# Rows of the residual stream for the second layer's out stage: 32x32 transposes on VectorE and SBUF transfers in place of TensorE transposes

## What is computed

```python
x = ffn_sublayer(x, mod_x, 0, norm_w[l, 0], ffn1_w_up[l], ffn1_w_down[l])
yx = modulated_norm(x, norm_w[l, 1], mod_x, 1)
px = split_projection(yx @ w_in[l])       # k, v, q, g, conv b/c/x, two gates
o_x = bidir_retention(qx, kx, vx, ret_log_decay[l], s_f, s_b)
# mixer_merge:
y_ret = (silu(g) * head_rmsnorm(o)) @ w_ret_out
y_conv = (conv_b * short_conv(conv_c * conv_x, conv_w)) @ w_conv_out
merged = sigmoid(gate_ret) * y_ret + sigmoid(gate_conv) * y_conv
x = x + mod_x[:, :, 5] * (merged @ w_out[l])
x = ffn_sublayer(x, mod_x, 2, norm_w[l, 2], ffn2_w_up[l], ffn2_w_down[l])
return rmsnorm(x, final_norm_w)
```

## Time and profile before

| | us |
|---|---|
| median of 3 runs (lowest, highest) | 2116.18 (2116.07, 2116.65) |
| profiled execution, its own time | 2116.01 |
| its span in the trace | 2114.2 |
| TensorE busy | 2105.1 |
| VectorE busy | 1442.1 |
| ScalarE busy | 805.6 |
| granted TensorE clock, share of full speed | 0.999 |

### The profile page before, as it was taken

How to read it: one execution, slowest core, us unless ns; L and a number is a source line. 1 busy time by engine, 2 the same in 40 slices (tenths; PEclk the granted TensorE clock), 3 DMA queues, 4 the chain that set the end, 5 groups by cost and what they waited for, 6 DMA issues and landing times.

```text
span 2114.2 us, 26101 instructions
## 1 busy us (share of the span) xinstructions
PE 2105.1 (100%) x10451; PEld 1782.0 (84%) x10451; DVE 1442.1 (68%) x1992; ACT 805.6 (38%) x1196; POOL 0.2 (0%) x4
## 2 busy tenths in 40 slices
PE   9999999999999999999999999999999999999998
PEld 7888888888888888898888888888888898888887
DVE  5687877668588773577777777733335688778765
ACT  5322222456322322342222233222223665557654
POOL 0000000000000000000000000000000000000000
PEclk9999999999999999999999999999999999999999
DMA  8665555431555653355555545433333446765664
GB/s 272 210 178 164 171 166 157 139 90 41 159 155 159 189 150 93 92 148 173 174 168 164 170 137 148 142 93 100 92 100 107 131 122 198 207 210 154 188 190 145
DMA packets 461628, 319.65 MB, mean 151 GB/s; under 512 B 19758, under 2 KB 436934, under 8 KB 461126
## 3 DMA queue, kind: packets, MB, share of 16 engines
q1 hardware_dynamic: 439708, 244.95, 40.5%
q10 hardware_dynamic: 21800, 73.03, 10.6%
HBM read 312.16 MB, written 1.05 MB: 148 GB/s over the span
## 4 chain that ended last, share of the span: by engine, by line
PE 99%; DVE 0%; ACT 0%; issue 0%; DVEq 0%
PE bank L657 22%; PE bank L659 22%; PE bank L658 22%; PE bank L668 9%; PE bank L671 5%; PE bank L990 4%; PE bank L696 2%; PE bank L734 1%; PE bank L754 1%; PE bank L753 1%; PE bank L752 1%; PE bank L700 1%; PE bank L738 1%; PE bank L1034 0%; PE bank L1035 0%; PE bank L1036 0%
## 5 line engine op out<-in xcount | busy, mean ns | idle before, releaser
L1606 DVE TENSOR_TENSOR LO<-RAW,HI 128x1024 fp32r<-128x1024 f32 (+1 forms) x431 | 518.3, 1207 | 358.7 <-ACT HI L1132 358.4
L657 PE MATMUL bank<-Y,HI 128*128 128x512 f32 (+1 forms) x1416 | 550.1, 388 | 0.0
L659 PE MATMUL bank<-Y,LO 128*128 128x512 f32 (+1 forms) x1416 | 549.2, 388 | 0.0
L658 PE MATMUL bank<-Y,HI 128*128 128x512 f32 (+1 forms) x1416 | 549.2, 388 | 0.0
L1132 ACT ACTIVATE HI<-RAW 128x1024 fp32r<-128x1024 f32 (+1 forms) x431 | 438.2, 1039 | 216.3 <-DMA RAW<-in_w_in_dram 58.2
L658 PEld LDWEIGHTS bank<-Y,HI 128*128 128x128 f32 x1416 | 265.9, 188 | 54.9 <-issue 0.5
L657 PEld LDWEIGHTS bank<-Y,HI 128*128 128x128 f32 x1416 | 265.9, 188 | 54.8 <-issue 0.5
L659 PEld LDWEIGHTS bank<-Y,LO 128*128 128x128 f32 x1416 | 265.9, 188 | 54.6
L1617 DVE SCALAR_TENSOR_TENSOR MODACC<-MODRAW,SC,MODACC 128x1024 f32<-128x1024 f32 x224 | 277.2, 1279 | 2.4 <-DMA MODRAW<-in_w_mod_dram 2.0
L1331 ACT ACTIVATE TMP<-bank 128x512 f32<-128x512 f32 x66 | 39.4, 598 | 414.9 <-PE bank L659 334.2
L668 PE MATMUL bank<-Y,HI 128*128 128x512 f32 x720 | 181.0, 393 | 0.0
(11 more groups left out here) (293 smaller groups left out, 2537.6 us busy)
## 6 DMA issues: line engine op xcount, KB each, us to landing
RAW<-in_ffn_w_up_dram SPq DMA_DIRECT2D x170, 512.0 KB, 4.1
MODRAW<-in_w_mod_dram ACTq DMA_DIRECT2D x128, 512.0 KB, 4.3
RAW<-in_w_in_dram SPq DMA_DIRECT2D x128, 512.0 KB, 4.1
RAW<-in_ffn_w_down_dram SPq DMA_DIRECT2D x66, 512.0 KB, 3.6
RAW<-in_ffn_w_down_dram SPq DMA_DIRECT2D x24, 384.0 KB, 3.2
WM<-in_w_mod_dram SPq DMA_DIRECT2D x16, 512.0 KB, 9.1
RAW<-in_w_ret_out_dram SPq DMA_DIRECT2D x16, 512.0 KB, 4.4
RAW<-in_w_conv_out_dram SPq DMA_DIRECT2D x16, 512.0 KB, 3.7
```

The lines of the kernel that those rows point to most:

```text
L657: mm(bank, hi, X[:, k, 0, cols], start=first, stop=False)
L658: mm(bank, hi, X[:, k, 1, cols], start=False, stop=False)
L659: return mm(bank, lo, X[:, k, 0, cols], start=False, stop=end)
L1606: V_.tensor_tensor(weights(v, 1), raw_weights(v), weights(v, 0).bitcast(F32), ALU.subtract).then_inc(lo_done, 1)
```

## The change

The transposes on TensorE and the four copies on ScalarE go. Instead VectorE transposes `H[:, n, 0:256]` within 32x32 blocks, in the conv stage behind the merge of each role-0 unit, into `turned` (spare columns of blocks 12 to 15 of `S`). A 32x32 transpose leaves each block in its own group of 32 partitions, so transfers must move it: 64 DMA transfers on SP's queue, each from one group of 32 partitions (q) to another (b), four ahead of the load of each gates unit from 8 to 23. They signal `rows_landed`, for which SP waits ahead of the load of the out stage's unit 7 (whose place overlaps `turned`), and VectorE at the start of the out stage.

```diff
-            if s.kind == "out":
-                s.ht = [p.acc(4 + i) for i in range(4)]
...
+        turned = spare(S, 12, 4).rearrange("p j a n -> p (j a) n")
+
+        def row_blocks(t, b, q, e):
+
+            src = turned[32 * q:32 * q + 32, :, (4 * t + b) * 32:(4 * t + b) * 32 + 32]
+            rows = spare(S, 16 + 2 * t, 2)[32 * b:32 * b + 32]
+            dst = rows.rearrange("p c a n -> p (c a) n")[:, :, P * e + 32 * q:P * e + 32 * q + 32]
+            return dst, src.rearrange("p (m e) n -> p e m n", e=2)[:, e, :, :]
...
+                        if s.kind == "out" and cc == 7:
+                            sp.wait_ge(rows_landed, 16 * 64)
                         load(s.u + cc, w.rearrange("(k p) n -> p k n", p=P)[:, cc:cc + 1, :])
...
+                        if s.wide and s.kind == "gates" and 8 <= cc < 24:
+                            if cc == 8:
+                                sp.wait_ge(blocks_turned, KT)
+                            for q in range(4):
+                                dst, src = row_blocks((cc - 8) // 8, (cc - 8) // 2 % 4, q, cc % 2)
+                                sp.dma_start(dst, src).then_inc(rows_landed, 16)
                         w, base = parts[cc % len(parts)]
                         load(s.u + cc, block_of(w, 0, KT, base + (cc // len(parts)) * P))
...
-                        if s.wide and cc in (8, 12, 16, 20):
-                            i = cc // 4 - 2
-                            a = follows(s).ht[i]
-                            bank_wait(pe, a)
-                            for m in range(4):
-                                ins = nc.tensor.transpose(B[a.bank][:, m * P:(m + 1) * P],
-                                                          H[:, 4 * (i % 2) + m, TCOLS[i // 2]], ident)
-                            ins.then_inc(ht_turned, 1)
...
-                        if s.wide and cc in (9, 13, 17, 21):
-                            i = cc // 4 - 2
-                            act.wait_ge(ht_turned, i + 1)
-                            a = follows(s).ht[i]
-                            A(xrow(i // 2, i % 2), halves2(B[a.bank][:]), ACT.Copy).then_inc(drained[a.bank], 1)
...
                     dve.wait_ge(dense, 2)
+                    dve.wait_ge(rows_landed, 16 * 64)
                     split_upto(nx.u + 3)
...
                             merge(s, cc, TMP[:, 0, HALF:2 * HALF])
+                            V_.transpose(turned[:, n, :], H[:, n, 0:NX]).then_inc(blocks_turned, 1)
```

More of the change, by code:

```diff
@@ L416, in build @@
         gates_set, gate_rows, final_landed = sem("gates_set"), sem("gate_rows"), sem("final_landed")
-        ht_turned, row_done, xrow_done, xsq_done, ssb_done = (
-            sem("ht_turned"), sem("row_done"), sem("xrow_done"), sem("xsq_done"), sem("ssb_done"))
+        blocks_turned, rows_landed, row_done, xrow_done, xsq_done, ssb_done = (
+            sem("blocks_turned"), sem("rows_landed"), sem("row_done"), sem("xrow_done"), sem("xsq_done"), sem("ssb_done"))
         xroot_done, xinv_done, xn_left, xn_right, xn_turned, scaled, dense = (
```

## The result

| | before | changed |
|---|---|---|
| median, us (lowest, highest; 7 runs each) | 2116.31 (2116.07, 2116.65) | 2122.71 (2121.14, 2122.88) |
| ratio (95% interval) | | 1.0028 (1.0019 to 1.0038) |
| span of the profiled execution, us | 2114.2 | 2120.9 |
| TensorE busy, us | 2105.1 | 2107.7 |

A forecast was written before the change was run, and what follows sets the result against it. TensorE, busy 2105.1 of 2114.2 us, was taken as the bound; 1.76 us saved on transposes and zero for all else gave 2114.4 us for the median, range 2113.8 to 2118.3.

The forecast's parts named there:

- The 0.44 us per group of transposes: Gates stage, TensorE: removing four groups of four transposes saves 4 x 0.44 = 1.76 us.
- rival D: TensorE's removed transposes save their full duration, 4.35 us, giving 2111.8 us; chance 0.02.
- The overbooking of SP: SP's queue, gates units 8 to 23: 3.22 us needed per unit of 2.79, overbooked by 0.43 us for 16 units.
- VectorE's transposes: Conv stage: eight added 128x256 transposes at 0.42 us each, covered by idle time or early LO; cost zero.
- the two new waits of SP and VectorE: Waits for all rows before the last out-stage load and VectorE's first out-stage weights: zero, over 25 us to spare.
- ScalarE's copies: Four removed PSUM copies of 0.58 us each on ScalarE, which waits for TensorE's banks there: counted as zero.
- The DMA share: Gates stage: share rises from 0.60 to 0.64 to 0.8 to 1.0, possibly lengthening landings by some tenths.
- Rival C: Each row transfer holds SP's queue until landed, 7.8 us per unit; TensorE stalls 71.5 us, 2185.9; chance 0.01.
- SP gains 2.2 us per unit: SP's queue behind gates unit 23: no rows queued, so out-stage loads from 1892 us on go out on time.
- a cover of 1.4 us: Gates unit 23: its load, 7.3 us late, still gives HI 1.4 us before TensorE wants it; no stall counted.
- rival A: Stall at gates unit 23 of 64p - 43.0 us, p per row issue 0.67 to 0.73: 2114.7 to 2118.4; chance 0.28.
- Rival B: Same place: SP blocks on its queue, p from 0.765; at 0.80 an 8.2 us stall, 2122.6 us; chance 0.09.

The follow-up runs named there:

- run 1: Changed kernel with the 64 row transfers replaced by 4 of 256 KB, same bytes, rows not the right ones: 2115.26 us, ratio 0.9994.
- run 3: Changed kernel with the same 64 transfers, three ahead of each load over gates units 8 to 29 instead of four: 2115.06 us, ratio 0.9994.
- run 6: Changed kernel with the same pieces joined into 32 transfers of twice the size, two ahead of each load: 2115.34 us, ratio 0.9994.
- run 7: Changed kernel with 32 joined transfers, two per load, and two H<-MODACC copies moved to the next up stage: 2114.94 us, ratio 0.9991.
- Run 9: Changed kernel with four transfers ahead of each load up to gates unit 15, then two from 16 to 31: 2118.93 us, ratio 1.0013.
- the repeat: The changed kernel measured once more, without any edit: 2122.03 us, ratio 1.0025.
- run 2: Changed kernel with 4 transfers of 256 KB and 60 of 8 KB in place of its 64: 2121.79 us, ratio 1.0026.
- run 4: Changed kernel with TensorE's 16 transposes and ScalarE's 4 copies put back, into unused space: 2122.83 us, ratio 1.003.

## Why the prediction was wrong

What held. The 0.44 us per group of transposes, 1.76 in all (runs 1, 3, 6 and 7, all by 1.76 in the gates); the full duration of rival D was never near. The overbooking of SP: 3.22 us per unit worked out, 3.20 measured. VectorE's transposes were hidden, the two new waits of SP and VectorE cost nothing, and TensorE gained nothing from ScalarE's copies beside the 1.76. The DMA share from 1846 to 1858 us rose from 0.63 only to 0.67, below the 0.8 to 1.0 that was expected, so there the engines were far from full. Rival C, a queue held to each landing, is excluded by 0.64 us from start to start against a landing of 3.0. The Trainium skill, "DMA: Bandwidth & Descriptors", § Issuing engines are not separate DMA queues, calls the time to start a DMA usually small relative to the DMA itself. One start is that here too (0.64 us against a landing of 3.0), but 64 of them on one queue decided the result.

What failed is the sentence "Behind unit 23 no more rows are queued, SP gains 2.2 us per unit, and the burst of out-stage loads from 1892 on finds it on time. So I count no stall, but from a cover of 1.4 us." Three things are wrong in it, in order of weight.

1. *The cover was measured at the wrong place.* I asked when TensorE wants unit 23. But between load and TensorE stands the loop of ScalarE and VectorE, in order, with every later HI, LO, merge and the whole of the out stage's Y, Z and LO behind it. In the kernel before it had no cover at its far end: its row in the table, 1.26 against 1.28, lies on the same line, though TensorE waits nowhere. Every further microsecond of the loop shows. VectorE's run at the start of the out stage has no gap: Y at 1903.95, four Z, four LO, and the rows' sums (L1769) right behind at 1914.18; in the changed kernel the same run goes from 1910.64 to 1920.87, 6.7 us later at both ends. Run 9 shows this alone: no stall in the gates, 4.14 us lost behind them. From VectorE's timelines, the kernel before (first line) and the changed one:

```profile
1914.18 0.69 DVE L1769 TENSOR_TENSOR PARTS<-bank,H 128x512 f32<-128x512 f32 x1
...
1910.64 1.22 DVE L1608 TENSOR_TENSOR Y<-XN,Y 128x1024 fp32r<-128x1024 f32 x1 [0.47 <-ACT Y L1139]
...
1920.87 0.68 DVE L1771 TENSOR_TENSOR PARTS<-bank,H 128x512 f32<-128x512 f32 x1
```

2. *That SP is on time again wins nothing back.* The prediction has no term for the loop of ScalarE and VectorE, whose busy shares of 38% and 68% look like room to catch up. The loop needs 11.4 us per group, TensorE 11.17. In the kernel before, a group with transposes lasted 11.17 + 0.44 = 11.61 on TensorE, and the loop fitted; the change took that away too. This is why 0.48 of the saving comes back in run 1, and not in run 7, which has two copies fewer in the loop. The gain of 2.2 us per unit for SP was too high as well: it was 1.4 (2.79 less 1.40), which SP still had time for.
3. *The load of unit 23 was 10.6 us late, not 7.3.* Three groups were held longer than 2.52 us: by 0.7, 1.5 and 1.0, together 3.2 us, nearly the whole difference. The mean per row issue became 0.69 us, inside rival A's span, by three outliers and not by a higher price of all. Landings were 4.6 us at the median (3.8 to 8.6) against 4.1 before.

With a mean of 0.69, rival A's formula gives a stall at unit 23 of 64 x 0.69 - 43.0 = 1.2 us, and with landings 0.5 longer 1.7: 2114.4 + 1.7 = 2116.1. With the 3.0 that TensorE really lost in the gates it is 2117.4. The range would have held both. It is the missing loop that makes 2122.7 of it. Rival B's outcome came, 2122.6 against 2122.7, but not at its price (p of 0.765 or more) nor at its place, a stall of 8 us at unit 23.

What the sum gives with the loop in it is an estimate from the changed kernel: the load of unit 23 may be late by some 3.1 us before the end moves (10.6 late, 7.47 lost against run 1; the repeat gives 3.1 in the same way, run 2 gives 3.2). The prediction's own 7.3 us of lateness would then have given 4.2 us against run 1, which is 2.9 slower than before, 2119. The long issues account for the rest, about one to one: over the normal 2.52 of a group they hold SP for 3.25 us in the changed kernel, 2.83 in its repeat and 4.77 in run 4, and the lateness of the loop less this is 4.2, 4.0 and 3.9.

Still open: what made some issues long. They stand at the same places in the changed kernel, its repeat and run 4: near 1816, 1823 and 1844 us, in run 4 at 1868 too. Beside all but the first lies a packet of the instruction queue, as in the DMA view of the changed kernel from 1823 to 1824 us (packets, MB, share of 16 engines):

```profile
q8 instruction: 1, 0.02, 9.8%
```

Such packets come at 1844, and in run 4 at 1845 and 1868, and nowhere else between 1812 and 1872. That is a coincidence in time; no run took them away. The one at 1816 has none beside it.

Another rival is the data. In the changed kernel the DMA share is 0.95 to 0.98 from 1816 to 1822 us, where the first long issue stands; 0.63 from 1826 to 1840, with none; and 1.05, as the profile counts it, from 1870 to 1881, where the loads back to back were held. Run 9 has 17 issues over 0.75 us, 15 of them between 1843 and 1880, most with no such packet beside them; its share is 0.68 from 1826 to 1843, with none, and 0.85 from 1845 to 1876. So a queue seems to be held when the DMA engines behind it are near full. No run was made to test this, and 3.2 of the 10.6 us of lateness hang on it.

## What to carry to other kernels

Slack at the engine that bounds a kernel is not slack of the chain that feeds it. When something is made late, follow it to the first loop of in-order engines that takes it over, and ask for that loop's own period, from the distance between repeats of one instruction, and not for the engines' busy shares: a loop at 11.4 us beside a bound of 11.17 keeps lateness to the end of the stage, and hands it on at the next one. And a queue that must also load weights has a budget of its own: count its issues per unit, at 0.64 us each here, and compare the sum with the unit. Below it they were free; a seventh above it (3.20 us against 2.79) they cost 0.3% of the kernel.

## What the runs showed of the hardware

- An issue on SP behind another cost 0.64 us from start to start, and its own time hardly depended on what it carried: at the median 0.591 us with 32 pieces (run 2), 0.601 with 128, 0.616 with 256 pieces of 1 KB (run 1), and with 256 pieces of 128 bytes 0.594 at the shortest and 0.658 at the median (run 6). Alone, a weight load took 0.37.
- Weight loads issued back to back held SP for up to 2.2 us each (1872 to 1879 us), more than the 0.59 behind a row transfer, at a DMA share of 1.05. So a late SP does not catch up at its shortest issue time.
- GpSimd's queue took its 64 issues at 0.54 us in bursts of seven with pauses of 2.3 to 6.0 us between, which the profile puts down to "issue".
- Rows of 128 bytes from SBUF to SBUF landed after 3.0 us at the median beside weight loads, where 8 KB of MRQ took 1.8.
